# Two transformer stacks on one core: the head norm of the second stack's attention, on VectorE whole or in pieces of 256 columns

## The chip, the core and the metric

One core of a Trainium2 chip runs the whole program. The metric is device time in microseconds (us), as a median of several executions. The engines are TensorE (PE in the profile; its weight loads are PEld), VectorE (DVE), ScalarE (ACT), GpSimd (POOL) and SyncE (SP), which issues most of the loads of weights.

## What is computed

Two stacks of two layers each work on 512 tokens of 1,024 features in fp32. The change touches only the attention of the second stack, which also carries 256 context tokens (in its first layer as queries and keys, in its last layer as keys alone):

```python
def diff_attn(q, k, v, lam):                      # 4 heads, each with two query/key halves of 64, values of 128
    s = jnp.einsum('bhqd,bhkd->bhqk', q, k).astype(jnp.float32) * (HEAD_DIM ** -0.5)
    a = jax.nn.softmax(s, axis=-1).reshape(b, N_HEADS, 2, nq, nk)
    w = a[:, :, 0] - lam * a[:, :, 1]
    return jnp.einsum('bhqk,bhkd->bhqd', w.astype(v.dtype), v)

def head_out(o, g_sub, lam_init):                 # the head norm
    o = rms_norm(o, g_sub) * (1.0 - lam_init)
...
        mix = jnp.concatenate([pool_mixer(u, w_pool[l], s_pool[l]),
                               head_out(o_att, g_subln[l], lam_init)], axis=-1)
        x = x + ga * (mix @ w_out[l])
```

## The kernel before

Activations lie with features on the 128 partitions and tokens along the columns: columns 0 to 255 are the context, 256 to 767 the tokens (`TC` = 256, `TA` = 768). Every large product is three passes of TensorE over a split of each operand into a high and a low part (lines L575 to L577). GpSimd splits each slab of weights in turn (L515 the high part, L518 the low part) as soon as TensorE has finished with the slab whose place it takes. The order on each engine is written by hand: every engine has an `attend2` of its own that walks the same list of units, and semaphores join them.

A unit is one head and one tile of 128 queries. The first layer of the second stack (L = 0) has 6 units for each of the 4 heads: two context tiles with 256 keys, then four token tiles with 768 keys. The last layer (L = 1) has only the four token tiles, so 4 units for each head. For a unit u the work is:

- TensorE computes the scores of both halves into PSUM banks 0 to 2 (L954). It may only do so once ScalarE has read the scores of unit u-1.
- VectorE takes the maximum, `maximum` (L2337), ScalarE the two exponentials (L1643, L1647).
- VectorE joins the two maps, `combine` (L2347 reciprocal of 2 sums, L2349, L2352).
- TensorE turns the map (L969), ScalarE copies it out (L1658: one copy for a 256-key map, two for a 768-key map, and in its order the second stands behind the exponentials of unit u+1), TensorE multiplies it with the values (L983).

Between these steps, in three slots for each unit, lies other work (`extra`, paced by `pace`): TensorE's projections of the next head's queries, keys and values into a ring of three PSUM banks, with their rotation. For the rotation TensorE swaps halves (L665) and VectorE multiplies and adds (`rope2`, L1937, L1939, L1942); the bank is free for the next projection only after L1942. VectorE has the window sums of the pool mixer there too (`centred_mean`, L2299 to L2324), and behind the last heads the low parts of the output's operand (`low`).

When the last unit of head n is multiplied, its head norm starts. ScalarE writes the output to `q_t[:, n]` and its square to `k_t[:, n]` (whose keys are no longer needed), TensorE sums the square over the partitions (L995), ScalarE takes the root into `k_t` (L1676: token columns first, then, for L = 0, the context columns). VectorE waits for the last root, takes the reciprocal of all columns (L2358) and multiplies (L2360). In VectorE's loop the head norm stands at the end of the iteration after the one in which the head ended: behind that unit's combination and its two later slots, ahead of the next maximum. Call the head's last unit e. VectorE's order is then

```python
maximum(e+1); combine(e+1); rest of the slots of e+1; head_norm; maximum(e+2); combine(e+2) ...
```

Nothing needs the result of the head norm until the output projection in the last head's slots, except for the last head, whose norm stands at the very end of the attention. There are 8 head norms: 4 of 768 columns (L = 0), 4 of 512 columns (L = 1).

Of the kernel before, what the change touches and what calls it, by code (L numbers as in the profile page):

```python
# [21 lines left out]
TA = TC + T  # L22
# [141 lines left out]
def steps2(head, last):  # L164

    return sum(STEPS2[kind] + (0 if last or kind not in "qu" else 4) for kind, m in TILES2[head])
# [32 lines left out]
def pace(steps, total, slots):  # L199

    done = 0
    for i in range(slots):
        for _ in range(done, (i + 1) * total // slots):
            next(steps)
        done = (i + 1) * total // slots
        if i == slots - 1:
            for _ in steps:
                pass
        yield
# [113 lines left out]
def program(nc, counts, a):  # L323
    tensor, vector, scalar, gpsimd, sync = nc.tensor, nc.vector, nc.scalar, nc.gpsimd, nc.sync
    scope = ExitStack()

    def signal(name, step=1):
        return Signal(nc, scope, name, counts, step)
# [16 lines left out]
    lams = top.take("lambda_columns", [P, 8])  # L345
# [60 lines left out]
    q_t = att2.take("q2", [P, NH2, TA])  # L406
    k_t = att2.take("k2", [P, NH2, TA])
# [43 lines left out]
    paired, inverted, scaled, h_lo = (signal(n) for n in ("squares_paired", "inverted", "scaled", "h_split"))  # L451
# [753 lines left out]
    def units2(last):  # L1205
        units = []
        for n in range(NH2):
            if not last:
                units += [(n, t, TC, 0) for t in range(2)]
            units += [(n, t, TA, 1) for t in range(2, TA // P)]  # L1210
        return units
# [572 lines left out]
    def vector_engine():  # L1784
# [458 lines left out]
        def second_layer(L):  # L2243
# [9 lines left out]
            rope2(L, 1, 0, 1)  # L2253
            rope2(L, 2, 0, 3)
            attend2(L, last, segs)
            outs = [(TC, TA, 1, TC)] if last else [(TC, TA, 1, TC), (0, TC, 2, 0)]
            vector.wait_ge(*mod_done.at(*(("up2", L - 1) if L else ("feed", DEPTH - 1))))
# [70 lines left out]
        def attend2(L, last, segs):  # L2328
            units = units2(last)
            per = len(units) // NH2  # L2330
            x0 = TC if last else 0
            ring = 0

            def maximum(u):
                n, t, nk, _ = units[u]
                vector.wait_ge(*scored.at(L, "2", u))
                vector.tensor_reduce(  # L2337
                    stat2[:, u % 4, 0:2],
                    psum[:, 0:2 * max(nk, 512)].rearrange("p (m k) -> p m k", m=2)[:, :, 0:nk],
                    AX.X, ALU.max, negate=True).then_inc(*maxed.up(L, "2", u))  # L2340

            def combine(u):
                n, t, nk, _ = units[u]
                rs, rr = stat2[:, u % 4, 2:4], stat2[:, u % 4, 4:6]
                e0, e1 = prob2[:, u % 2, 0:nk], second2[:, 0:nk]
                vector.wait_ge(*probs.at(L, "2", u))
                vector.reciprocal(rr, rs).then_inc(*inverted.up(L, "2", u))  # L2347
                vector.wait_ge(*inverted.at(L, "2", u))
                vector.tensor_scalar(e1, e1, rr[:, 1:2], lams[:, 5:6], ALU.mult,  # L2349
                                     ALU.mult).then_inc(*dve_misc.up(L, "second_map", u))  # L2350
                vector.wait_ge(*dve_misc.at(L, "second_map", u))
                vector.scalar_tensor_tensor(out=e0, in0=e0, scalar=rr[:, 0:1], in1=e1, op0=ALU.mult,  # L2352
                                            op1=ALU.add).then_inc(*normed.up(L, "2", u))

            def head_norm(n):
                ho, rms = q_t[:, n, x0:TA], k_t[:, n, x0:TA]
                vector.wait_ge(*rooted.at(L, "head", n, 0))
                vector.reciprocal(rms, rms).then_inc(*inverted.up(L, "head", n))  # L2358
                vector.wait_ge(*inverted.at(L, "head", n))
                vector.scalar_tensor_tensor(out=ho, in0=ho, scalar=lams[:, 6:7], in1=rms, op0=ALU.mult,  # L2360
                                            op1=ALU.mult).then_inc(*scaled.up(L, "head", n))

            def low(k):
                vector.wait_ge(*o_hi.at(L, "2", k))
# [54 lines left out]
            ended = []  # L2419
            for s in range(len(units) + 1):  # L2420
                if s % per == 0 and s < len(units):
                    n = s // per
                    fill = pace(extra(n), steps2(n, last), 3 * per)
                if s < len(units):
                    maximum(s)
                for part in range(3):
                    next(fill, None)
                    if part == 0 and s < len(units):
                        combine(s)
                while ended:  # L2430
                    head_norm(ended.pop())
                if s and units[s - 1][3] and units[s - 1][1] == TA // P - 1:
                    ended.append(units[s - 1][0])
            while ended:
                head_norm(ended.pop())
            low(7)

        angles()
# [142 lines left out]
```

## Time and profile before

| what | value |
|---|---|
| median of 3 runs | 3588.51 us (3586.37 to 3588.83) |
| the profiled execution | 3586.86 us, its span in the trace 3585.5 us |
| PE busy | 3408.4 us, 95% of the span |
| POOL, DVE, ACT busy | 1578.2, 1323.7 and 800.8 us |
| mean granted clock of TensorE | 0.982 |

The span runs from the first to the last instruction; 1.4 us of the execution lie outside it. A busy time counts the instructions of one engine, which overlap with those of the others. The attention of the second stack runs from about 2040 to 2300 us (L = 0) and from about 2960 to 3170 us (L = 1).

### The profile page before, as it was taken

What the parts mean: (1) busy time and instruction counts of PE and PEld (TensorE: products, weight loads), DVE (VectorE), ACT (ScalarE), POOL (GpSimd) and SP (SyncE); (2) the same over time, 40 slices, a digit from 0 to 9 for tenths busy, and PEclk for the clock granted to TensorE, in tenths of its full rate; (3) what the DMA queues carried; (4) which work ended last, traced back from release to release, by engine and by line L of the source; (5) the groups of instructions that cost most, each with busy time, mean ns of one, the idle gap of its engine ahead of it and who ended that gap; (6) DMA issues with size and microseconds to landing.
All of it is one profiled execution on the core that took longest, in us unless ns stands there. A gap on an engine that the chain in (4) does not pass through costs nothing.

```text
span 3585.5 us, 42527 instructions
## 1 busy us (share of the span) xinstructions
PE 3408.4 (95%) x17440; PEld 2687.4 (75%) x17452; DVE 1323.7 (37%) x2282; ACT 800.8 (22%) x1608; POOL 1578.2 (44%) x996
## 2 busy tenths in 40 slices
PE   6989999999999999999999898889999989889998
PEld 4667777788866677777778787778888878667886
DVE  5843313311159333132122665641211255551113
ACT  2243411100022444111011334320110123420111
POOL 3413356566544134664565421233333333235664
PEclk8999999999999999999999999999999999999999
DMA  6434122333233441335442210132432311114321
GB/s 203 135 127 143 48 90 94 106 94 94 84 99 124 130 130 48 94 103 161 130 141 83 81 48 24 37 106 71 141 118 95 106 51 59 36 47 138 97 94 59
DMA packets 403370, 346.80 MB, mean 97 GB/s; under 512 B 9701, under 2 KB 400613, under 8 KB 403178
## 3 DMA queue, kind: packets, MB, share of 16 engines
q1 hardware_dynamic: 395328, 336.62, 30.0%
q10 hardware_dynamic: 7850, 7.47, 0.7%
q8 instruction: 139, 2.28, 0.3%
q14 instruction: 53, 0.43, 0.0%
HBM read 341.96 MB, written 2.10 MB: 96 GB/s over the span
## 4 chain that ended last, share of the span: by engine, by line
PE 88%; DVE 6%; ACT 3%; issue 1%; DMA 1%; POOL 1%; ACTq 0%; DVEq 0%; POOLq 0%
PE psum L575 26%; PE psum L577 25%; PE psum L576 25%; PE psum L557 2%; PE psum L837 2%; PE psum L983 1%; PE psum L954 1%; PE psum L825 1%; PE psum L769 1%; DVE psum L1838 1%; PE psum L665 1%; DVE k L2358 1%; PE psum L812 1%; PE psum L810 1%; PE psum L814 1%
## 5 line engine op out<-in xcount | busy, mean ns | idle before, releaser
L515 POOL TENSOR_SCALAR weights_hi<-raw_weights 128x1024 fp32r<-128x1024 f32 (+3 forms) x496 | 498.0, 1004 | 1937.1 <-PE psum L577 1617.7
L575 PE MATMUL psum<-h_hi,weights_hi 128*128 128x512 f32 (+1 forms) x2832 | 1139.5, 402 | 70.0 <-DVE h_lo L1880 54.2
L518 POOL TENSOR_TENSOR weights_lo<-raw_weights,weights_hi 128x1024 fp32r<-128x1024 f32 (+3 forms) x496 | 1089.0, 2196 | 41.4
L577 PE MATMUL psum<-h_hi,weights_lo 128*128 128x512 f32 (+1 forms) x2832 | 1077.8, 381 | 0.0
L576 PE MATMUL psum<-h_lo,weights_hi 128*128 128x512 f32 (+1 forms) x2832 | 1076.3, 380 | 0.0
L575 PEld LDWEIGHTS psum<-h_hi,weights_hi 128*128 128x128 f32 x2832 | 538.8, 190 | 230.7 <-issue 111.1
L576 PEld LDWEIGHTS psum<-h_lo,weights_hi 128*128 128x128 f32 x2832 | 538.9, 190 | 117.1 <-issue 15.6
L577 PEld LDWEIGHTS psum<-h_hi,weights_lo 128*128 128x128 f32 x2832 | 537.9, 190 | 109.0
L575 PE MATMUL psum<-hidden_hi,weights_hi 128*128 128x512 f32 (+1 forms) x1120 | 411.7, 368 | 0.0
L576 PE MATMUL psum<-hidden_lo,weights_hi 128*128 128x512 f32 (+1 forms) x1120 | 411.3, 367 | 0.0
L577 PE MATMUL psum<-hidden_hi,weights_lo 128*128 128x512 f32 (+1 forms) x1120 | 410.8, 367 | 0.0
L2135 DVE SCALAR_TENSOR_TENSOR x<-psum,mod,x 128x512 f32<-128x512 f32 (+1 forms) x184 | 123.3, 691 | 559.2 <-PE psum L577 559.1
L575 PEld LDWEIGHTS psum<-hidden_hi,weights_hi 128*128 128x128 f32 x1120 | 211.4, 189 | 37.7 <-issue 0.8
L577 PEld LDWEIGHTS psum<-hidden_hi,weights_lo 128*128 128x128 f32 x1120 | 211.3, 189 | 36.3
L576 PEld LDWEIGHTS psum<-hidden_lo,weights_hi 128*128 128x128 f32 x1120 | 211.4, 189 | 36.1
L1616 ACT ACTIVATE relu_squared<-psum 128x256 f32<-128x256 f32 (+1 forms) x96 | 47.1, 525 | 661.9 <-PE psum L577 661.9
L2271 DVE TENSOR_TENSOR psum<-psum,relu_squared 128x256 f32<-128x256 f32 (+1 forms) x96 | 58.4, 610 | 330.6 <-ACT relu_squared L1616 328.9
L557 PE MATMUL psum<-raw_weights,cond 128*32 128x256 f32 x1536 | 109.7, 408 | 22.5 <-DVE cond L1796 13.8
L2150 DVE TENSOR_TENSOR silu<-psum,silu 128x512 f32<-128x512 f32 x44 | 30.4, 692 | 200.2 <-ACT silu L1497 200.2
L1497 ACT ACTIVATE silu<-psum 128x512 f32<-128x512 f32 x44 | 26.4, 599 | 339.7 <-PE psum L577 339.7
L1250 ACT ACTIVATE squares<-x 128x512 f32<-128x512 f32 (+1 forms) x80 | 43.3, 563 | 244.1 <-DVE x L2135 210.8
L557 PEld LDWEIGHTS psum<-raw_weights,cond 128*32 128x32 f32 x1536 | 42.6, 114 | 72.8 <-issue 41.0
(284 smaller groups left out, 3599.3 us busy)
## 6 DMA issues: line engine op xcount, KB each, us to landing
raw_weights<-in_ada_w SPq DMA_DIRECT2D x96, 1024.0 KB, 5.3
raw_weights<-in_w_mlp SPq DMA_DIRECT2D x64, 1024.0 KB, 5.2
raw_weights<-in_w_in SPq DMA_DIRECT2D x54, 1024.0 KB, 5.4
raw_weights<-in_w_ffn_in SPq DMA_DIRECT2D x88, 512.0 KB, 5.2
raw_weights<-in_w_out SPq DMA_DIRECT2D x16, 1024.0 KB, 5.0
raw_weights<-in_w_ffn_out SPq DMA_DIRECT2D x16, 1024.0 KB, 5.0
raw_weights<-in_w_in SPq DMA_DIRECT2D x30, 512.0 KB, 4.2
raw_weights<-in_w_branch SPq DMA_DIRECT2D x56, 128.0 KB, 2.2
```

The costliest lines, as they stand in the source:

```text
L515: gpsimd.tensor_scalar(whi[:, r, c0:c1], raw[:, raw_slot, c0:c1], 1.0, 1.0, ALU.mult, ALU.mult).then_inc(*split_hi.up(*key, half))
L518: gpsimd.tensor_tensor(wlo[:, r, c0:c1], raw[:, raw_slot, c0:c1], whi[:, r, c0:c1].bitcast(F32), ALU.subtract).then_inc(*split.up(*key, half))
L557: ins = tensor.matmul(bank[bk][32 * g:32 * g + 32, 0:256], cond[:, 4 * kk + g, at:at + 32], view[:, 4 * kk + g, :], start=c == 0 and kk == ...
L575: tensor.matmul(out, sh, mh, start=first, stop=False, skip_group_check=shared)
L576: tensor.matmul(out, sh, ml, start=False, stop=False, skip_group_check=shared)
L577: return tensor.matmul(out, sl, mh, start=False, stop=last, skip_group_check=shared)
L665: tensor.matmul(bank[bk][:, 0:n], matrix, x, start=True, stop=True).then_inc(*swapped.up(*key))
L837: ins = tensor.matmul(bank[3][:, i * P:i * P + P], values_of(kind, h // 2)[:, j, :], probt[:, q, j * P:j * P + P], start=j == 0, stop=j == i)
L1250: scalar.activation(part_of(work, 1 + (k + 1) % 2 if k else 0, x0, x1), X[:, k, x0:x1], ACT.Square, scale=scale).then_inc(*squared.up(whic ...
L1616: scalar.activation(sq2[:, count % 2, 0:c1 - c0], bank[bk][:, 0:c1 - c0], ACT.Relu).then_inc(*moved.up(L, "relu2", chunk, n, s))
L2135: vector.scalar_tensor_tensor(out=xs, in0=bank[bk][:, at:at + x1 - x0], scalar=mod[:, part * 8 + n, m:m + 1], in1=xs, op0=ALU.mult, op1=AL ...
L2271: vector.tensor_tensor(x, x, sq2[:, count % 2, 0:c1 - c0], ALU.mult).then_inc(*dve_misc.up(L, "square", count))
```

## The change

The reciprocals and multiplications of a head norm are cut into pieces of 256 columns: three for L = 0, two for L = 1. `head_norm` becomes a generator, and VectorE's loop takes steps of it, two steps in each of the second and third slots of a unit, behind the slot's other work. The generator does all reciprocals first, then all multiplications. For the last head nothing follows, and all pieces are made in a row at the end.

```diff
             def head_norm(n):
-                ho, rms = q_t[:, n, x0:TA], k_t[:, n, x0:TA]
+                cuts = [(c, c + 256) for c in range(x0, TA, 256)]
                 vector.wait_ge(*rooted.at(L, "head", n, 0))
-                vector.reciprocal(rms, rms).then_inc(*inverted.up(L, "head", n))
-                vector.wait_ge(*inverted.at(L, "head", n))
-                vector.scalar_tensor_tensor(out=ho, in0=ho, scalar=lams[:, 6:7], in1=rms, op0=ALU.mult,
-                                            op1=ALU.mult).then_inc(*scaled.up(L, "head", n))
+                for c0, c1 in cuts:
+                    rms = k_t[:, n, c0:c1]
+                    vector.reciprocal(rms, rms).then_inc(*inverted.up(L, "head", n, c0))
+                    yield
+                for c0, c1 in cuts:
+                    ho, rms = q_t[:, n, c0:c1], k_t[:, n, c0:c1]
+                    vector.wait_ge(*inverted.at(L, "head", n, c0))
+                    vector.scalar_tensor_tensor(out=ho, in0=ho, scalar=lams[:, 6:7], in1=rms, op0=ALU.mult,
+                                                op1=ALU.mult).then_inc(*scaled.up(L, "head", n))
+                    if c1 < TA:
+                        yield
+
+            def head_step():
+                if ended and next(ended[0], "done") == "done":
+                    ended.pop(0)
...
                     next(fill, None)
                     if part == 0 and s < len(units):
                         combine(s)
-                while ended:
-                    head_norm(ended.pop())
+                    else:
+                        head_step()
+                        head_step()
                 if s and units[s - 1][3] and units[s - 1][1] == TA // P - 1:
-                    ended.append(units[s - 1][0])
+                    ended.append(head_norm(units[s - 1][0]))
             while ended:
-                head_norm(ended.pop())
+                head_step()
             low(7)
```

The other engines' orders are the same. VectorE has 24 more instructions in the program. The first place is VectorE at the end of head 0 in L = 0, where `q_108` and `k_109` are `q_t` and `k_t`. Before:

```order
L2352 SCALAR_TENSOR_TENSOR maps<-maps,softmax_stats_106,second_map 128x256
L1937 TENSOR_TENSOR psum<-psum,axial_sin 128x512
L1939 TENSOR_TENSOR q_108<-q_108,axial_cos 128x512
L1942 TENSOR_TENSOR q_108<-psum,q_108 128x512
L2358 RECIPROCAL k_109<-k_109 128x768
L2360 SCALAR_TENSOR_TENSOR q_108<-q_108,lambda_columns,k_109 128x768
L2337 TENSOR_REDUCE softmax_stats_106<-psum 128x2
L2347 RECIPROCAL softmax_stats_106<-softmax_stats_106 128x2
L2349 TENSOR_SCALAR second_map<-second_map,softmax_stats_106,lambda_columns 128x768
L2352 SCALAR_TENSOR_TENSOR maps<-maps,softmax_stats_106,second_map 128x768
L2337 TENSOR_REDUCE softmax_stats_106<-psum 128x2
```

And now, at the same place:

```order
L2360 RECIPROCAL k_109<-k_109 128x256 x2
L1937 TENSOR_TENSOR psum<-psum,axial_sin 128x512
L1939 TENSOR_TENSOR q_108<-q_108,axial_cos 128x512
L1942 TENSOR_TENSOR q_108<-psum,q_108 128x512
L2360 RECIPROCAL k_109<-k_109 128x256
L2365 SCALAR_TENSOR_TENSOR q_108<-q_108,lambda_columns,k_109 128x256
L2337 TENSOR_REDUCE softmax_stats_106<-psum 128x2
L2347 RECIPROCAL softmax_stats_106<-softmax_stats_106 128x2
L2349 TENSOR_SCALAR second_map<-second_map,softmax_stats_106,lambda_columns 128x768
L2352 SCALAR_TENSOR_TENSOR maps<-maps,softmax_stats_106,second_map 128x768
L2365 SCALAR_TENSOR_TENSOR q_108<-q_108,lambda_columns,k_109 128x256 x2
L2337 TENSOR_REDUCE softmax_stats_106<-psum 128x2
```

All three reciprocals and one multiplication still stand ahead of the next maximum, two of the reciprocals now ahead of the rotation; two multiplications stand behind the next combination, ahead of the maximum after that.

The second place is VectorE at the end of head 0 in L = 1. Before:

```order
L2352 SCALAR_TENSOR_TENSOR maps<-maps,softmax_stats_106,second_map 128x768
L1937 TENSOR_TENSOR psum<-psum,axial_sin 128x512
L1939 TENSOR_TENSOR k_109<-k_109,axial_cos 128x512
L1942 TENSOR_TENSOR k_109<-psum,k_109 128x512
L2299 TENSOR_TENSOR windows<-pool_in 128x799
L2307 TENSOR_TENSOR windows<-windows 128x797
L2358 RECIPROCAL k_109<-k_109 128x512
L2360 SCALAR_TENSOR_TENSOR q_108<-q_108,lambda_columns,k_109 128x512
L2337 TENSOR_REDUCE softmax_stats_106<-psum 128x2
```

And now:

```order
L2352 SCALAR_TENSOR_TENSOR maps<-maps,softmax_stats_106,second_map 128x768
L2360 RECIPROCAL k_109<-k_109 128x256 x2
L1937 TENSOR_TENSOR psum<-psum,axial_sin 128x512
L1939 TENSOR_TENSOR k_109<-k_109,axial_cos 128x512
L1942 TENSOR_TENSOR k_109<-psum,k_109 128x512
L2299 TENSOR_TENSOR windows<-pool_in 128x799
L2307 TENSOR_TENSOR windows<-windows 128x797
L2365 SCALAR_TENSOR_TENSOR q_108<-q_108,lambda_columns,k_109 128x256 x2
L2337 TENSOR_REDUCE softmax_stats_106<-psum 128x2
```

Here all four pieces still stand ahead of the next maximum, the reciprocals ahead of the rotation of the keys instead of behind it. It is the same for heads 1 and 2 of L = 1, but that the rotation of head 1 is still ahead of the reciprocals. For heads 1 and 2 of L = 0 three reciprocals and one multiplication stand ahead of the next maximum and two multiplications behind the next combination.

## Rows read from the trace of the kernel before

**Rows 1.** The page: busy time, share of the span and instructions of each engine.

```profile
PE 3408.4 (95%) x17440; PEld 2687.4 (75%) x17452; DVE 1323.7 (37%) x2282; ACT 800.8 (22%) x1608; POOL 1578.2 (44%) x996
```

**Rows 2.** Timeline, TensorE alone: start, duration, instruction, idle time before and its releaser.

```profile
2133.38 1.56 PE L954 MATMUL psum<-k,q 64*128 64x256 f32 x8 [1.88 <-ACT second_map L1647]
2140.46 0.39 PE L575 MATMUL psum<-weights_hi,h_hi 128*128 128x256 f32 x1 [1.19 <-DVE k L1942]
2191.95 1.56 PE L954 MATMUL psum<-k,q 64*128 64x256 f32 x8 [3.64 <-ACT second_map L1647]
2200.14 1.60 PE L983 MATMUL psum<-map_t,v 128*128 128x128 f32 x12 [1.53 <-ACT map_t L1658]
2245.45 2.93 PE L954 MATMUL psum<-k,q 64*128 64x256 f32 x8 [6.36 <-ACT second_map L1647]
3051.66 2.93 PE L983 MATMUL psum<-map_t,v 128*128 128x128 f32 x12 [4.13 <-ACT map_t L1658]
3099.72 1.61 PE L983 MATMUL psum<-map_t,v 128*128 128x128 f32 x12 [2.96 <-ACT map_t L1658]
```

**Rows 3.** VectorE's groups by form, 2000 to 3200 us: busy, mean ns.

```profile
L2358 DVE RECIPROCAL k<-k 128x768 f32<-128x768 f32 x4 | 19.8, 4952 | 11.8 <-ACT k L1676 11.8
L2358 DVE RECIPROCAL k<-k 128x512 f32<-128x512 f32 x4 | 13.4, 3346 | 7.3 <-ACT k L1676 7.3
```

**Rows 4.** Timeline around the end of head 0, L = 0.

```profile
2120.91 0.48 DVE L2352 SCALAR_TENSOR_TENSOR maps<-maps,softmax_stats,second_map 128x256 f32<-128x256 f32 x1
...
2121.82 0.47 ACT L1676 ACTIVATE k<-psum,eps 128x256 f32<-128x256 f32 x1
...
2123.66 4.94 DVE L2358 RECIPROCAL k<-k 128x768 f32<-128x768 f32 x1
2128.64 1.02 DVE L2360 SCALAR_TENSOR_TENSOR q<-q,lambda_columns,k 128x768 f32<-128x768 f32 x1
2129.57 1.75 DVE L2337 TENSOR_REDUCE softmax_stats<-psum 128x2 f32<-128x1536 f32 x1
...
2135.06 1.68 DVE L2352 SCALAR_TENSOR_TENSOR maps<-maps,softmax_stats,second_map 128x768 f32<-128x768 f32 x1
...
2136.02 2.97 POOL L518 TENSOR_TENSOR weights_lo<-raw_weights,weights_hi 128x1024 fp32r<-128x1024 f32 x1
...
2136.66 1.74 DVE L2337 TENSOR_REDUCE softmax_stats<-psum 128x2 f32<-128x1536 f32 x1
...
2139.71 0.69 DVE L1942 TENSOR_TENSOR k<-psum,k 128x512 f32<-128x512 f32 x1
```

**Rows 5.** Timeline, VectorE, around the ends of heads 1 and 2, L = 0.

```profile
2195.68 1.75 DVE L2337 TENSOR_REDUCE softmax_stats<-psum 128x2 f32<-128x1536 f32 x1
...
2239.76 1.97 DVE L2360 SCALAR_TENSOR_TENSOR q<-q,lambda_columns,k 128x768 f32<-128x768 f32 x1
```

**Rows 6.** Timeline around the end of head 0, L = 1.

```profile
3034.51 2.55 POOL L518 TENSOR_TENSOR weights_lo<-raw_weights,weights_hi 128x1024 fp32r<-128x1024 f32 x1
...
3034.88 3.00 DVE L2352 SCALAR_TENSOR_TENSOR maps<-maps,softmax_stats,second_map 128x768 f32<-128x768 f32 x1
...
3037.80 0.69 DVE L1937 TENSOR_TENSOR psum<-psum,axial_sin 128x512 f32<-128x512 f32 x1
...
3038.86 2.71 POOL L518 TENSOR_TENSOR weights_lo<-raw_weights,weights_hi 128x1024 fp32r<-128x1024 f32 x1
...
3040.03 2.38 DVE L2299 TENSOR_TENSOR windows<-pool_in 128x799 f32<-128x799 f32 x1
...
3040.17 0.19 PEld L575 LDWEIGHTS psum<-weights_hi,h_hi 128*128 128x128 f32 x1 [0.19 <-DVE k L1942]
...
3047.41 1.75 DVE L2337 TENSOR_REDUCE softmax_stats<-psum 128x2 f32<-128x1536 f32 x1
```

**Rows 7.** Busy times by stretch: from:to, length, PE, PEld, DVE, ACT, POOL, PEclk, DMA.

```profile
2192.00:2196.00 4.00, 4.00 (x21) 3.14 (x22) 3.82 (x6) 0.49 (x2) 0.00 (x0) 1.00 0.00 0
3051.70:3057.20 5.50, 5.50 (x20) 4.30 (x20) 1.30 (x2) 0.18 (x1) 0.00 (x0) 0.50 0.00 0
```

## The prediction

> **What bounds the kernel now.** I read the page first: TensorE is busy 95% of the span, so a change on VectorE counts only where TensorE waits for it [rows 1]. Then I read TensorE's timeline behind the end of each head and looked at what it waited for. Six head norms stand inside the loop (heads 0 to 2 of both layers). Behind five of them TensorE waits for something that the late maximum holds up [rows 2]:
>
> - L = 0, head 0: 1.88 us for the scores' banks, then 1.19 us for a PSUM bank that the keys' rotation frees.
> - L = 0, head 1: 3.64 us and 1.53 us. L = 0, head 2: 6.36 us.
> - L = 1, head 0: 4.13 us for the second copy of a map, which stands behind the exponentials on ScalarE. L = 1, head 1: 2.96 us. Behind head 2 there is no such wait.
>
> At each place the question is when the next maximum starts, and what else in VectorE's queue now starts later.
>
> **Prices of the pieces.** A reciprocal takes 4.952 us for 768 columns and 3.346 for 512 [rows 3]: 1.606 us for 256 columns and 0.13 us fixed, so a piece takes 1.74 us. An instruction starts about 0.08 us before the one ahead of it ends (2128.64 + 1.02 against 2129.57) [rows 4], so pieces follow each other every 1.66 us. A multiplication of 256 columns has the form of the combination that took 0.48 us [rows 4], so 0.40 us each in a row. The whole norm of L = 0 took 2129.57 - 2123.66 = 5.91 us [rows 4]; in pieces it is 3 x 1.66 + 3 x 0.40 = 6.18, that is 0.27 us more. For L = 1, 3.35 + 0.75 less the overlaps is 4.05 us; 2 x 1.66 + 2 x 0.40 = 4.12, that is 0.07 more. The gap between the dependent reciprocal and multiplication is gone, which pays for part of it. The other side of the trade is an old warning of the Trainium skill, page "VectorE: DVE Perf Modes", sections "The TRN2 errata" and "Rules for kernel authors": minimise the number of VectorE instructions, since each pays a fixed cost (58 cycles in its table, 0.06 us; about 150 by its own measurement, 0.16 us). By that, 24 more instructions would cost an estimated 1.5 to 3.7 us of VectorE; the two forms measured here give 0.13 us each before the overlap, and my sum goes by them.
>
> **L = 0, head 0.** The root of the context columns ends at 2122.29 [rows 4]. Before, the rotation ran first and the norm began at 2123.66. Now two reciprocals run from 2122.33 to 2125.65, the rotation (2.0 us, as the one from 2138.40 to 2140.40) to 2127.65, one reciprocal and one multiplication (2.06 us) to 2129.7. The maximum starts at 2129.7 against 2129.57: nothing won. Behind the next combination, which ends at 2136.74, stand the two other multiplications. Here lies the one large term. Both inputs of a multiplication are in SBUF, and where GpSimd is in an instruction such a one stands still: with L518 running from 3034.51, a combination took 3.00 us, where the same shape takes 1.02 [rows 4, 6]. GpSimd's L518 was issued at 2136.02, while VectorE was in its combination, and ended at 2138.99 [rows 4]. It is in line first, so I take it to run first: the multiplications end at 2139.8, and the maximum that started at 2136.66 starts 3.1 us later. The rotation of the keys behind it ended at 2140.40 and TensorE waited for it [rows 2, 4]: TensorE's wait of 1.19 us becomes 4.3 us. That is longer than the 4.13 that brought the half clock, so I add one stretch, 2.7 us. Term: +3.1 and +2.7. If VectorE goes first, it is 0.8 + 0.1 = +0.9 and no stretch.
>
> **L = 0, heads 1 and 2.** Three reciprocals and one multiplication stand ahead of the maximum: 5.38 against 5.91, so it is 0.53 us earlier and the first wait shrinks by that. Then the two multiplications (0.80 us) stand ahead of the maximum after it, which VectorE starts without idling already (2195.68) [rows 5], and from which the second wait (1.53) hangs: +0.27. The same for head 2, where the longer multiplication (1.97 us) met GpSimd and the shorter will too [rows 5]: +0.27. Sum +0.5.
>
> **L = 1, head 0.** The reciprocals move ahead of the keys' rotation. The rotation started at 3037.80 and ends 3.3 us later now, at 3043.2. TensorE needed its bank and started as soon as it was free, at 3040.17 [rows 6], so it stops there for 3.1 us more. This lies ahead of the wait of 4.13 us and is paid out of it. Meanwhile GpSimd's L518, from 3038.86, had held the first window sum (2.38 us, where 768 columns at the same rate take 1.02) and a little of the rotation (2.3 us to TensorE's start at 3040.17, in place of 2.0) [rows 4, 6]; 3.3 us later both miss it, which gives back 1.4 + 0.3 less the pieces' 0.07, so 1.6 us: the maximum starts at about 3045.8 in place of 3047.41. TensorE, 3.1 us late, would reach its product with the values at 3047.53 + 3.05 = 3050.6, when the map is there: 1.1 us earlier than 3051.66. And the 4.13 us have become one wait of some 3.2 us, under the 3.64 that kept the full clock, so this half-clock stretch goes. Term: -1.1 and -2.7. If the clock falls at 3.2 us after all, TensorE works slowly up to the product and it is +1.6 in place of -3.8.
>
> **L = 1, heads 1 and 2, and the last heads.** All pieces are ahead of the maximum: +0.07 each, +0.1. The last heads' pieces cost 0.27 and 0.07 us; TensorE has the products of six other operand rows in between, so 0, at most +0.4. Signals and waits of the pieces are VectorE's own. No DMA, no slab and no other engine's order is moved.
>
> **Sum.** 3.1 + 2.7 + 0.5 - 1.1 - 2.7 + 0.1 = +2.6 us. The profiled execution took 3586.86 us, so 3589.5; it lay 1.65 us under the median of the three runs, and the median becomes 3588.5 + 2.6 = 3591.1 us. The three runs differ by 2.5 us, and 0.2% (7.2 us) is about what a measurement of this kernel can tell from no change.
>
> **Rivals.**
>
> 1. *The pieces free the maximum.* VectorE idles between each maximum and its combination, while ScalarE makes the exponentials; if the norm lay in such gaps the 21.7 us of waits and two stretches of 2.7 us would go: 3588.5 - 27 = 3561 us. Against it: the order shows 5.38 of 6.18 us still ahead of the next maximum in L = 0, and all of it in L = 1. Something like half would need the order to be other than it is. Chance 0.04.
> 2. *The rotation's bank starves TensorE.* The place is L = 1, head 0: TensorE stops at 3040 for 3.2 us, and if the clock falls there, the sum is 3.1 + 2.7 + 0.5 + 1.6 + 0.1 = +8.0, 3596.5 us, slower than before. It decides from an idle time between 3.64 us (full clock) and 4.13 us (half), so a rotation 0.5 us later than I think is enough. For it: two reciprocals now stand ahead of every rotation that shares their slots. Against it: the 3.64 of [rows 2]. Chance 0.13.
> 3. *VectorE goes before GpSimd at head 0 of L = 0.* Then +0.9 and no stretch there: 0.9 + 0.5 - 3.8 + 0.1 = -2.3, 3586.2 us. For it: its multiplications are queued directly behind the combination. Against it: in 2136.02 to 2138.99 GpSimd's instruction was waiting already. The Trainium skill, page "SBUF — State Buffer", section "SBUF: two separate sides", says that whichever starts first has the shared ports for its whole instruction and the other is blocked; by that the case is decided by who is issued first, which is GpSimd. Chance 0.15.
> 4. *Nothing of the large terms*: the holds and stretches shift against each other and only the pieces' fixed costs stay, +0.6, 3589.1 us. Chance 0.2.
>
> The forecast has 0.48. **How the numbers follow.** The forecast, rivals 3 and 4 lie within 0.2%. Rival 1 is faster, with some 0.01 for scatter; rival 2 is just above the bound, and part of it falls below. So faster 0.05, same 0.83, slower 0.12. The range goes from rival 3 less the scatter of the runs (3584) to rival 2 and a little (3598).
>
> **What would show it.** Right: reciprocals of 1.74 us; the maximum at the end of head 0 (L = 0) no earlier against the scores than before; a multiplication of some 2.7 us there, a wait of some 4 us for the rotation, and the half clock behind it; in L = 1, head 0, a wait of 3 us in front of the value tile and the full clock at the products with the values. Wrong: if the six first waits shrink by more than 1 us each; if the multiplications at 2136 take 0.48 us; if the rotations' banks hold TensorE at a place where it had no wait; if moved GpSimd instructions meet other VectorE ones, which I worked out only at these places.

## The result, and the profile after

The changed kernel takes 3592.72 us, the median of 20 executions (3591.53 to 3594.55); the kernel before took 3587.27 us beside it (20 executions, 3585.01 to 3589.47). The ratio is 1.0016, with a 95% interval of 1.0009 to 1.0022: 5.45 us more. That is less than the 7.2 us (0.2%) that the prediction took as the bound of "same". The interval lies above 1, so with this many executions the loss is real. The profiled execution took 3593.38 us with a span of 3592.1, against 3586.86 and 3585.5.

One thing in the listing of the order ahead of the prediction must be put right. A head's last unit e is multiplied with the values while VectorE is at unit e+1, so the norm stood behind the combination of e+2 and ahead of `maximum(e+3)`, one unit later than that listing says. The rows of the order and the prediction's steps show it rightly.

The page, first line of its busy times:

```profile
PE 3415.7 (95%) x17440; PEld 2694.0 (75%) x17452; DVE 1322.0 (37%) x2306; ACT 800.1 (22%) x1608; POOL 1578.2 (44%) x996
```

TensorE has the same 17,440 instructions as in [rows 1] and is busy 7.3 us longer: it is slower in places, it does not do more. VectorE has its 24 additional instructions and is busy no longer.

TensorE's timeline of the changed kernel at the places of [rows 2] (start, duration, instruction, idle time before and its releaser):

```profile
2133.74 1.56 PE L954 MATMUL psum<-k,q 64*128 64x256 f32 x8 [1.84 <-ACT second_map L1647]
2143.80 0.58 PE L575 MATMUL psum<-weights_hi,h_hi 128*128 128x256 f32 x1 [4.15 <-DVE k L1942]
2196.83 2.93 PE L954 MATMUL psum<-k,q 64*128 64x256 f32 x8 [2.88 <-ACT second_map L1647]
2205.82 1.60 PE L983 MATMUL psum<-map_t,v 128*128 128x128 f32 x12 [0.74 <-ACT map_t L1658]
2250.56 2.93 PE L954 MATMUL psum<-k,q 64*128 64x256 f32 x8 [5.83 <-ACT second_map L1647]
2261.39 1.85 PE L1022 MATMUL psum<-pool_in,ada_rows 128*128 128x512 f32 x2 [2.23 <-ACT map_t L1658]
3051.82 0.39 PE L575 MATMUL psum<-weights_hi,h_hi 128*128 128x256 f32 x1 [3.01 <-DVE k L1942]
3104.47 1.60 PE L983 MATMUL psum<-map_t,v 128*128 128x128 f32 x12 [1.59 <-ACT map_t L1658]
```

Line by line against [rows 2]: the scores' wait at head 0 is as it was (1.88, now 1.84), the keys' rotation is waited for 4.15 in place of 1.19 us, the scores of heads 1 and 2 wait 0.76 and 0.53 us less, head 1's second wait is 0.79 us shorter (1.53, now 0.74), a wait of 2.23 us stands where head 2 had one of 0.56 (below), and in L = 1 a wait of 3.01 us for a rotation's bank has come in front of the value tile while the one of 4.13 us is gone. The products behind the waits of 2.88 and 5.83 us show the duration of the half clock (2.93 us for eight scores, against 1.56).

VectorE's groups by form, 2000 to 3200 us, for [rows 3] (busy, mean ns):

```profile
L2360 DVE RECIPROCAL k<-k 128x256 f32<-128x256 f32 x20 | 33.5, 1719 | 20.0 <-ACT k L1676 20.0
L2365 DVE SCALAR_TENSOR_TENSOR q<-q,lambda_columns,k 128x256 f32<-128x256 f32 x20 | 11.6, 614 | 0.0
```

The piece of a reciprocal takes 1.72 us, as worked out (1.74). The 20 pieces are busy 33.5 us, where the 8 whole reciprocals took 33.2. The multiplications have a mean of 614 ns where 480 were expected: some are held.

VectorE and GpSimd at the end of head 0, L = 0, for [rows 4]:

```profile
2122.73 3.37 DVE L2360 RECIPROCAL k<-k 128x256 f32<-128x256 f32 x2 [0.93 <-ACT k L1676]
...
2127.98 1.74 DVE L2360 RECIPROCAL k<-k 128x256 f32<-128x256 f32 x1
...
2129.94 1.75 DVE L2337 TENSOR_REDUCE softmax_stats<-psum 128x2 f32<-128x1536 f32 x1
...
2136.44 2.97 POOL L518 TENSOR_TENSOR weights_lo<-raw_weights,weights_hi 128x1024 fp32r<-128x1024 f32 x1
...
2137.08 3.01 DVE L2365 SCALAR_TENSOR_TENSOR q<-q,lambda_columns,k 128x256 f32<-128x256 f32 x2
...
2140.01 1.74 DVE L2337 TENSOR_REDUCE softmax_stats<-psum 128x2 f32<-128x1536 f32 x1
...
2143.05 0.69 DVE L1942 TENSOR_TENSOR k<-psum,k 128x512 f32<-128x512 f32 x1
```

The maximum starts at 2129.94, 0.37 us later than before, which is how much later the whole attention began: nothing won. Two multiplications of 256 columns take 3.01 us together; the second starts at 2139.61, just after L518 has ended (2139.41), so the first was held by 2.1 us. The maximum behind them starts at 2140.01 against 2136.66.

End of head 0 in L = 1, for [rows 6]:

```profile
3043.15 2.55 POOL L518 TENSOR_TENSOR weights_lo<-raw_weights,weights_hi 128x1024 fp32r<-128x1024 f32 x1
3043.52 3.00 DVE L2352 SCALAR_TENSOR_TENSOR maps<-maps,softmax_stats,second_map 128x768 f32<-128x768 f32 x1
...
3046.44 3.35 DVE L2360 RECIPROCAL k<-k 128x256 f32<-128x256 f32 x2
...
3049.71 0.67 DVE L1937 TENSOR_TENSOR psum<-psum,axial_sin 128x512 f32<-128x512 f32 x1
...
3051.68 0.98 DVE L2299 TENSOR_TENSOR windows<-pool_in 128x799 f32<-128x799 f32 x1
...
3054.39 1.75 DVE L2337 TENSOR_REDUCE softmax_stats<-psum 128x2 f32<-128x1536 f32 x1
```

The window sum takes 0.98 us, where L518 had held it for 2.38. The maximum starts 6.98 us later than in [rows 6], and the maximum ahead of it 8.61 us later (3033.01 against 3024.40): 1.6 us given back, as in the prediction.

The row of before that answers to the one at 2261.39, TensorE's timeline of the kernel before:

```profile
2255.49 1.10 PE L1022 MATMUL psum<-pool_in,ada_rows 128*128 128x512 f32 x2 [0.56 <-ACT map_t L1658]
```

The granted clock in two stretches, for [rows 7] (the seventh value behind the time is PEclk):

```profile
2143.80:2149.00 5.20, 5.20 (x24) 5.20 (x25) 5.06 (x11) 0.50 (x2) 0.00 (x0) 0.50 0.00 0
3051.80:3058.00 6.20, 6.18 (x52) 6.19 (x53) 6.09 (x9) 2.41 (x6) 0.00 (x0) 1.00 0.39 137
```

Behind the wait of 4.15 us the clock is at half, behind the one of 3.01 us it is full.

### The profile page after: what moved, and what is told of

Same layout as the page of the kernel before. It is cut to its first block, busy times and chain, and to the rows that moved or that the text cites. A ratio compares the mean times of both kernels' runs of the same rounds, so it can differ in the third digit from the quotient of the medians.

```text
span 3592.1 us, 42551 instructions
## 1 busy us (share of the span) xinstructions
PE 3415.7 (95%) x17440; PEld 2694.0 (75%) x17452; DVE 1322.0 (37%) x2306; ACT 800.1 (22%) x1608; POOL 1578.2 (44%) x996
## 4 chain that ended last, share of the span: by engine, by line
PE 88%; DVE 5%; ACT 3%; issue 1%; DMA 1%; POOL 1%; ACTq 0%; DVEq 0%; SPq 0%; POOLq 0%
PE psum L575 26%; PE psum L577 25%; PE psum L576 25%; PE psum L557 2%; PE psum L837 2%; PE psum L983 1%; PE psum L954 1%; PE psum L825 1%; PE psum L769 1%; DVE psum L1838 1%; PE psum L665 1%; PE psum L812 1%; PE psum L810 1%; DVE k L2360 1%; PE psum L814 1%
## 5 line engine op out<-in xcount | busy, mean ns | idle before, releaser
L518 POOL TENSOR_TENSOR weights_lo<-raw_weights,weights_hi 128x1024 fp32r<-128x1024 f32 (+3 forms) x496 | 1088.5, 2195 | 41.4
L2154 DVE TENSOR_TENSOR psum<-psum,silu 128x512 f32<-128x512 f32 x44 | 30.8, 700 | 179.8 <-PE psum L577 179.6
```

The costliest lines, as they stand in the source:

```text
L518: gpsimd.tensor_tensor(wlo[:, r, c0:c1], raw[:, raw_slot, c0:c1], whi[:, r, c0:c1].bitcast(F32), ALU.subtract).then_inc(*split.up(*key, half))
```

## The experiments

Each kernel is the changed one with the edit shown. Times are medians; the kernel before ran beside them, 3587.86 us for the first four and 3587.28 for `cut_in_place`, `mult_whole`, `gaps` and `gap_whole`. `gaps` has 5 executions, `gap_whole` 6, the other six 11. To say where time went I use one measure throughout: the start of the same unit's maximum (L2337, 40 of them) in two traces. The difference of these shifts over a head is what the head cost. A trace is one execution, though, and need not lie at the median: those of `whole_early` and `cut_in_place` lie 4.0 us above theirs (1.4 and 2.4 us of shift are there ahead of the first maximum), that of `l1_pieces` 2.9 us below (1.5 of it ahead of the first maximum). So a head's cost says what happened there once, and the medians say what a kernel costs.

**L = 0 alone, L = 1 alone** (`l0_pieces`; `l1_pieces` has 1 and 0 exchanged):

```diff
-                cuts = [(c, c + 256) for c in range(x0, TA, 256)]
+                cuts = [(c, c + 256) for c in range(x0, TA, 256)] if L == 0 else [(x0, TA)]
...
-                    else:
+                    elif L == 0:
                         head_step()
                         head_step()
+                while ended and L != 0:
+                    head_step()
```

> Pieces in L = 0 only, the norms of L = 1 whole and at their old place. Theory (the change is a sum of local terms: +5.2 us at head 0 of L = 0 from multiplications that stand still behind GpSimd and the half clock after it, about 0 at head 1, +1.9 at head 2, -4.1 at head 0 of L = 1): this kernel is 7.1 us slower than before, and the wait of 4.1 us at head 0 of L = 1 with its half clock is back. Rival (half of the change's 5.5 us lies outside the attention, in where the instructions or loads fall): 9 to 10 us slower, or the markers behind 3200 us shift by more than those of the attention.

> Pieces in L = 1 only, the norms of L = 0 as before. Theory of local terms: 3.9 us faster than before (-4.1 at head 0 from the wait in front of the value tile in place of the longer one behind it, +0.2 at head 1, 0 at head 2), with the full clock at the products with the values. Rival of an outside cost: only 1 to 2 us faster or no change.

Measured: 3594.34 us (1.0018, 1.0009 to 1.0027), +6.5; and 3587.03 us (0.9998, 0.9989 to 1.0007), -0.8. Together +5.7, and the whole change has +5.45, so the medians add up, within intervals of some 3 us to either side. The loss is all in L = 0. With whole norms in L = 1 the old wait is back (3059.30, 4.14 us, with a 2.93 us product). In `l1_pieces` head 0 gave back 2.5 us by the maxima, not 3.8, because the wait that should have kept the full clock did not:

```profile
3041.63 0.39 PE L575 MATMUL psum<-weights_hi,h_hi 128*128 128x256 f32 x1 [2.98 <-DVE k L1942]
```

```profile
3041.63:3045.63 4.00, 4.00 (x21) 4.00 (x22) 3.96 (x5) 0.44 (x1) 0.00 (x0) 0.57 0.63 221
```

The same wait for the same bank as at 3051.82 above (2.98 and 3.01 us), once with half the clock behind it and once with all of it. For `l1_pieces` 3.9 us less was expected and the rival had 1 to 2 us or nothing; by its number the rival came out. The trace has 1.6 us of the difference at this place, by the clock, and 1.2 us behind the attention in code that is the same, which is what the rival named.

**The whole norm, only earlier** (`whole_early`):

```diff
-                cuts = [(c, c + 256) for c in range(x0, TA, 256)]
+                cuts = [(x0, TA)]
```

> One cut of all columns with the change's stepping: the norm is whole but stands in the second slot, ahead of the rotation that the third slot brings. Theory (cutting costs 0.3 us a norm, the place is what counts): the gain of about 4 us at head 0 of L = 1 is there too if the 3.8 us wait for the rotation's bank keeps the full clock, and in L = 0, with no multiplication behind the combination, head 0 loses 1 to 2 us; in total 2 to 4 us faster than the change. Rival (a wait of 3.8 us brings the half clock): the gain at head 0 of L = 1 is 1 us or less.

Measured: 3589.72 us (1.0005, 0.9996 to 1.0014), 3.0 us under the changed kernel, as expected, but not by the steps expected. L = 0, head 0, costs 5.2 us here too (1 to 2 were expected), though no multiplication stands behind a combination. The norm sits ahead of the queries' rotation, and TensorE waits 2.21 us for it. The combination then meets L518 and takes 2.99 us, and an instruction of the keys' rotation meets the next L518 and takes 1.72 in place of 0.68. TensorE waits 2.92 us for that rotation, and the clock behind is half (0.50 for 5 us):

```profile
2136.19 2.54 POOL L518 TENSOR_TENSOR weights_lo<-raw_weights,weights_hi 128x1024 fp32r<-128x1024 f32 x1
2136.55 2.99 DVE L2352 SCALAR_TENSOR_TENSOR maps<-maps,softmax_stats,second_map 128x768 f32<-128x768 f32 x1
...
2140.55 2.37 POOL L518 TENSOR_TENSOR weights_lo<-raw_weights,weights_hi 128x1024 fp32r<-128x1024 f32 x1
...
2141.74 1.72 DVE L1939 TENSOR_TENSOR k<-k,axial_cos 128x512 f32<-128x512 f32 x1
...
2144.31 0.58 PE L575 MATMUL psum<-weights_hi,h_hi 128*128 128x256 f32 x1 [2.92 <-DVE k L1942]
```

So what the norm costs there is a question of which instruction stands where L518 starts, not of the cut. In L = 1 neither the theory nor its rival held: the wait for the rotation's bank at head 0 is 3.75 us, the clock behind it is half (0.55 over 3.7 us), and head 0 still gave back 1.8 us, not 4 and not under 1.

**All pieces ahead of the next maximum** (`all_ahead`):

```diff
-                        head_step()
-                        head_step()
+                        for _ in range(3):
+                            head_step()
```

> As the change, but three steps in each slot, so that in L = 0 too every piece stands ahead of the next maximum and nothing behind the next combination. Theory (the large loss at head 0 of L = 0 is the hold by GpSimd and the half clock): its wait for the keys' rotation returns to 1 to 2 us at full clock, the loss there is about 1 to 2 us instead of 5.2, and the kernel is 3 us faster than the change or more. Rival (the rotation behind three reciprocals costs as much, since TensorE waits for its bank, or head 1's first wait grows to 3.9 us and brings the half clock): within 1 us of the change.

Measured: 3591.78 us (1.0010, 1.0001 to 1.0019), 0.9 us under the changed kernel, a difference that the two intervals do not tell from nothing; the theory wanted 3 us. Its step at head 0 of L = 0 held: that head costs 1.4 us in place of 5.3, with a wait of 1.77 us at the full clock, so the two multiplications behind the combination are the large term there. But head 2 costs 3.1 us, since all three now meet GpSimd:

```profile
2240.20 2.34 POOL L518 TENSOR_TENSOR weights_lo<-raw_weights,weights_hi 128x1024 fp32r<-128x1024 f32 x1
2241.29 5.18 DVE L2365 SCALAR_TENSOR_TENSOR q<-q,lambda_columns,k 128x256 f32<-128x256 f32 x3
...
2243.80 2.39 POOL L518 TENSOR_TENSOR weights_lo<-raw_weights,weights_hi 128x1024 fp32r<-128x1024 f32 x1
...
2250.19 2.93 PE L954 MATMUL psum<-k,q 64*128 64x256 f32 x8 [9.48 <-ACT second_map L1647]
```

The one multiplication of 768 columns took 1.97 us here [rows 5]; three of 256 take 5.18 (1.53, 1.25 and 2.56 us), because the last of them reaches into the second L518 as well, and the wait of 6.36 us becomes 9.48.

**The cut alone, at the old place** (`cut_in_place`), and **reciprocals in pieces, the multiplication whole** (`mult_whole`, with three steps for each slot as above):

```diff
-                    else:
-                        head_step()
-                        head_step()
+                while ended:
+                    head_step()
```

```diff
...
-                for c0, c1 in cuts:
-                    ho, rms = q_t[:, n, c0:c1], k_t[:, n, c0:c1]
-                    vector.wait_ge(*inverted.at(L, "head", n, c0))
+                ho, rms = q_t[:, n, x0:TA], k_t[:, n, x0:TA]
+                vector.wait_ge(*inverted.at(L, "head", n, TA - 256))
...
```

> The pieces of the change, all in a row at the old place of the norm, in both layers. This is the price of the cutting alone. Theory: 0.27 us a norm in L = 0 and 0.07 us in L = 1 where TensorE waits, plus what GpSimd holds the two further multiplications at head 2 of L = 0 (up to 3 us, as 5.2 us for three of them in the kernel with all pieces ahead): 1 to 4 us slower than before, with no new wait for a rotation. Rival (the order of pieces and rotation is of no matter, the pieces themselves cost the 5 us): 5 us slower or more.

> As the kernel with all pieces ahead of the next maximum, but the multiplication of a norm whole. Theory (each cut multiplication is a chance to stand still behind GpSimd): at head 2 of L = 0 the multiplication takes 1 to 2 us in place of 5.2 us for three, TensorE's wait of 9.5 us there falls to 6 to 7 us, and the kernel is about 3 us faster than that one. Rival: the wait there stays above 9 us.

Measured: 3590.09 us (1.0007, 0.9999 to 1.0016) and 3589.92 us (1.0009, 1.0000 to 1.0017). The cut alone costs 2.8 us, inside the 1 to 4 expected. With it head 2 of L = 0 costs 3.1 us by the maxima (the same 5.18 us of held multiplications, the same wait of 9.48 us), head 2 of L = 1 costs 0.8, and the other four between +0.3 and -0.3: more instructions cost next to nothing but where they are held. With the multiplication whole, head 2 costs 0.0 us and TensorE waits 6.36 us again. That settles the 5.18 us: it is the number of multiplications in front of GpSimd, not their place. The whole one starts 1.21 us behind the start of L518, the first of the three 1.09 and 1.10 us behind it.

```profile
2243.75 1.95 DVE L2364 SCALAR_TENSOR_TENSOR q<-q,lambda_columns,k 128x768 f32<-128x768 f32 x1
```

But `mult_whole` is only 1.9 us faster than `all_ahead`, where 3 were expected, and in its trace other heads lose by the clock. Head 0 of L = 0 costs 2.9 us (a wait of 2.08 us for the keys' rotation, and 0.57 of the clock over 4 us behind it). Head 1 costs 1.1 us: its scores waited 3.64 us, to the hundredth as in the kernel before, and had half the clock where that had all of it [rows 7].

```profile
2194.79 2.93 PE L954 MATMUL psum<-k,q 64*128 64x256 f32 x8 [3.64 <-ACT second_map L1647]
```

```profile
2194.79:2200.20 5.41, 5.41 (x14) 3.75 (x15) 5.23 (x7) 0.12 (x1) 0.00 (x0) 0.50 0.00 0
```

**The two kernels once more** (`change_again`, `before_again`), unaltered, for the clock:

> The changed kernel once more, unaltered, for the clock alone. Its first profile showed at the end of L = 0, head 0, a wait of 4.15 us for the keys' rotation with half the clock behind it, one of 2.88 us at head 1 with half the clock, and one of 3.01 us at L = 1, head 0, with the full clock. Theory A: the wait's length decides, so the clocks are the same as in the first profile at every place. Theory B: for a wait of 2 to 4 us the clock that follows also depends on the execution, so at least one of the waits of about 3 us comes with the other clock than the first time, by 1.3 to 2.7 us of time at the place. The order, the waits' lengths and the starts of the maxima up to the first such place repeat within 0.1 us in both.

> The kernel before once more, unaltered, for the clock alone. Its first profile showed waits of 3.64 us (L = 0, head 1) with the full clock, 6.36 (head 2) and 4.13 us (L = 1, head 0) with half the clock, and 2.96 us (L = 1, head 1) with the full clock. Theory A, the wait's length decides: the same clocks. Theory B, it depends on the execution too for waits of 2 to 4 us: the 3.64 or the 2.96 may come with half the clock, and the span differs from 3585.5 by about as much as the places with another clock make, 1.3 to 2.7 us each.

Measured: 3592.54 and 3588.07 us, one execution each. TensorE's timeline and clock in the second execution of the changed kernel:

```profile
3049.47 0.56 PE L575 MATMUL psum<-weights_hi,h_hi 128*128 128x256 f32 x1 [2.99 <-DVE k L1942]
...
3103.38 2.26 PE L983 MATMUL psum<-map_t,v 128*128 128x128 f32 x12 [2.85 <-ACT map_t L1658]
```

```profile
3049.50:3055.50 6.00, 6.00 (x38) 6.00 (x39) 5.90 (x9) 2.25 (x4) 0.00 (x0) 0.72 0.41 144
```

The waits of L = 0 have the same lengths within 0.01 us and the same clocks as the first time (half behind 4.15, 2.87 and 5.82 us), but for the last, which is 2.04 us in place of 2.23 and again has half the clock behind it. In L = 1 the 2.99 us have half the clock behind them, where 3.01 us had the full one. That took 1.5 us at head 0 (-2.5 by the maxima, -4.0 in the first execution). At head 1 the wait is 2.85 us in place of 1.59, the products take 2.26 us in place of 1.60, and another 1.6 us go. In the kernel before, the second execution has the same clocks as the first; its wait of 3.64 us (3.61 now) kept the full clock both times. So for waits of about 3 us the length does not decide the clock: theory B holds for the changed kernel. The kernel before alone shows nothing against either, but the 3.64 us of `mult_whole` had half the clock, so up to there at least the length does not decide. The Trainium skill, page "TensorE: Matmul & The Clock Gate", section "Part 1: The HAM clock gate", says of a kernel's first products that the moment of the transition depends on where they fall in the gate's own timing, which does not start anew with the kernel. No run here shows that timing; one wait with either clock behind it does not contradict it.

**The pieces between a maximum and its combination** (`gaps`), where VectorE waits for the exponentials, by a small table: key is (last layer, head 2, place, iterations since the head ended), value the number of steps. "gap" is ahead of `combine(s)` in the first slot, "end" behind the last slot.

```diff
+            plan = {(False, False, "gap", 2): 1, (False, False, "gap", 3): 1, (False, False, "gap", 4): 1,
+                    (False, False, "gap", 5): 3,
+                    (False, True, "end", 1): 1, (False, True, "gap", 2): 1, (False, True, "gap", 3): 4,
+                    (True, False, "gap", 1): 1, (True, False, "gap", 2): 1, (True, False, "gap", 3): 2,
+                    (True, True, "gap", 1): 1, (True, True, "gap", 2): 3}
...
                     if part == 0 and s < len(units):
+                        head_step(s, "gap")
                         combine(s)
-                    else:
-                        head_step()
-                        head_step()
+                head_step(s, "end")
```

and **the whole norm in one such gap** (`gap_whole`), with `cuts = [(x0, TA)]` and

```diff
+            plan = {(False, False, "gap", 2): 2, (False, True, "gap", 2): 2,
+                    (True, False, "gap", 1): 2, (True, True, "gap", 1): 2}
```

> The same pieces, placed by a table: one reciprocal in each gap between a maximum and its combination (VectorE idles 1.9 us and more there for the exponentials), the multiplications in one gap after them; for head 2 of L = 0 one reciprocal at the old place. Theory (TensorE's waits behind the heads come from what stands between a combination and the next maximum, and a piece in the other gap is free): the 21.7 us of waits shrink to 5 us or less and the half-clock stretches at heads 2 of L = 0 and 0 of L = 1 go, so 15 to 25 us faster than before, 3562 to 3573 us. Rival (the combination is as much on the path as the maximum, or the pieces meet GpSimd): less than 8 us faster.

> As the kernel with the gaps, but each norm whole in one gap between maximum and combination. Theory (a reciprocal of 5 us does not fit a gap of 1.9 us and makes the combination 4 us late, which TensorE's next turning of a map waits for): 5 to 15 us slower than the kernel with pieces in the gaps, between that and before. Rival (cutting is of no use, only the gap is): within 2 us of the kernel with pieces in the gaps.

Measured: **3571.62 us (0.9956, 0.9942 to 0.9969)**, 15.7 us under the kernel before, and 3576.76 us (0.9971, 0.9959 to 0.9982), 10.5 us under it. Both beat both kernels. The time of `gaps` is in the range expected (15 to 25 us less), that of `gap_whole` too (5 to 15 us above `gaps`). TensorE's waits of over 1 us that are left in `gaps` in the stretches of [rows 2]:

```profile
2141.30 0.38 PE L575 MATMUL psum<-weights_hi,h_hi 128*128 128x256 f32 x1 [3.07 <-DVE k L1942]
...
2198.55 1.60 PE L983 MATMUL psum<-map_t,v 128*128 128x128 f32 x12 [1.22 <-ACT map_t L1658]
...
2238.58 1.56 PE L954 MATMUL psum<-k,q 64*128 64x256 f32 x8 [1.11 <-ACT second_map L1647]
2241.49 0.66 PE L969 MATMUL psum<-constants,maps 128*128 128x128 f32 x4 [1.35 <-DVE maps L2352]
2244.60 0.47 PE L575 MATMUL psum<-h_hi,weights_hi 128*128 128x512 f32 x1 [2.46 <-DVE h_lo L2395]
```

9.2 us in place of 21.7 (5 or less were expected), and in L = 1 none but those that the kernel before has too and that the 21.7 leaves out (1.92 and 1.91 us, and 5.35 where it has 4.39). By the maxima the heads of L = 0 give +1.5, -4.0 and -2.1 us, those of L = 1 -6.7, -3.2 and -0.8. Head 0 of L = 0 does not gain: its maximum starts at 2125.93 in place of 2129.57 and the scores no longer wait, but GpSimd's slab then starts as the combination does (L518 at 2133.19, L2352 at 2133.55 for 3.00 us in place of 1.68), and the keys' rotation is late again, with 3.07 us of waiting and part of the stretch behind it at half the clock (0.65 over 4.8 us). In `gap_whole` a norm of 768 columns is longer than the gap. At head 2 it pushes the combination into GpSimd, and TensorE waits 5.25 us for the map:

```profile
2241.59 1.25 DVE L2365 SCALAR_TENSOR_TENSOR q<-q,lambda_columns,k 128x768 f32<-128x768 f32 x1
2242.12 2.92 POOL L518 TENSOR_TENSOR weights_lo<-raw_weights,weights_hi 128x1024 fp32r<-128x1024 f32 x1
...
2242.95 2.51 DVE L2349 TENSOR_SCALAR second_map<-second_map,softmax_stats,lambda_columns 128x768 f32<-128x768 f32 x1
...
2246.57 1.11 PE L969 MATMUL psum<-constants,maps 128*128 128x128 f32 x4 [5.25 <-DVE maps L2352]
```

By the maxima the two kernels are alike in L = 1 (-6.7, -3.2 and -0.9 us in `gap_whole`). In L = 0 `gap_whole` has +2.2, -1.9 and -0.9. So the gap is worth two thirds of the gain, and the pieces, once they lie in gaps, another 5.1 us; in the two traces 4 of them lie in L = 0, where the norm is longest.

## Why the prediction was right, and where its terms were not

The forecast was +2.6 us and 3591.1; the medians differ by 5.45 us and the median is 3592.72. It came out as "same" and inside the range, by the mechanism foreseen: nearly all of the norm still ahead of the next maximum, multiplications held at head 0 of L = 0, a hold and a half-clock stretch saved at head 0 of L = 1. The sum was half of what the medians show. Two terms were mis-sized. Ahead of, between and behind the attentions, where the sum had nothing, 3.3 us lie in the first execution and -0.4 in the second. By the maxima, in us:

| place | forecast | first execution | second |
|---|---|---|---|
| ahead of the first maximum | 0 | +0.4 | -0.9 |
| L = 0, head 0 | +5.8 | +5.3 | +5.6 |
| L = 0, head 1 | +0.27 | 0.0 | 0.0 |
| L = 0, head 2 | +0.27 | +1.9 | +1.8 |
| between the two attentions | 0 | +1.0 | -0.2 |
| L = 1, head 0 | -3.8 | -4.0 | -2.5 |
| L = 1, heads 1 and 2 | +0.1 | +0.1 | +1.2 |
| from the first maximum to the last | +2.6 | +4.3 | +5.9 |
| behind the last maximum | 0 | +1.9 | +0.7 |
| the whole span | +2.6 | +6.6 | +5.7 |

- **The pieces' prices** were right (1.72 against 1.74 us), and so, within 0.25 us, were the starts of the maxima: 0.0 at head 0 (+0.1 foreseen), 0.7 and 0.5 us earlier at heads 1 and 2 (0.53 foreseen; waits 0.76 and 0.53 us shorter). The warning against more instructions did not bite: `cut_in_place` loses over 0.3 us at two of six places only, at the larger one through GpSimd, and in the changed kernel the reciprocals are busy 0.3 us longer with 12 more of them (33.5 against 33.2).
- **L = 0, head 0.** The mechanism came as foreseen: held multiplications (3.1 us later maximum foreseen; 2140.01 - 2136.66 less the 0.4 of the start is 3.0), 4.15 us of waiting (4.3 foreseen), half the clock behind. Rival 3, that VectorE goes first, is excluded.
- **L = 0, head 1.** The late multiplications cost nothing: the shorter second wait (0.74 in place of 1.53) takes in the half clock that now follows the 2.88 us. That half clock was not foreseen.
- **L = 0, head 2**: mis-sized, +1.9 in place of +0.27. I stopped at the maximum. It is 0.25 us later, as worked out, but the map that hangs from it was already just in time. Before, TensorE ran on half the clock for some 6.2 us behind the scores' wait; now for some 4.2 us behind the shorter one, so it gets to the map first, waits 2.23 us and falls to half once more (two products of 512 columns in 1.85 in place of 1.10 us). What is late next was to be asked once more.
- **L = 1, head 0**: the step that failed is "under the 3.64 that kept the full clock, so this half-clock stretch goes". The wait was 3.0 us as foreseen, but one row of 3.64 us with the full clock is no threshold: the same wait of 3.0 us had the full clock in one execution of this kernel and half of it in another, and half in `l1_pieces`. Rival 2 named this and drew its line between 3.64 and 4.13 us, which was wrong in place but right in kind. The term is -4.0 or -2.5 by execution, and head 1 goes with it (+0.2 or +1.6). That the first execution met the forecast here is luck as far as the traces tell: of the six traces with the reciprocals or the norm ahead of this rotation (waits of 2.98 to 3.79 us) it alone kept the full clock, and in the others the head gave back 0.6 to 2.5 us.
- **Rival 1**, the pieces in the gap, would have been 27 us. The order excluded it for this change, and the kernel that does it gains 15.7.

The +1.0 between the attentions, where the kernels are the same, is absent in the second execution. Of the time behind the last maximum 0.3 and 0.1 us are there by 3200 us, for the last head's pieces the forecast allowed 0 to 0.4; the rest comes by 3250 us, in code that is the same. There the clock was at half for 10.2 us in the first execution (3210.5 to 3220.7) and for 6.8 us in the second and in the kernel before. Against the kernel before in its own two executions (spans of 3585.5 and 3586.8 us) the two spans lie 5.5 us higher on average, as the medians do. How often each clock occurs at 3050 us was not counted.

## What to carry to other kernels

Cutting an instruction helps only if the pieces lie where their engine idles: look up the idle stretch (here between maximum and combination) and put them there, since a place "behind the next step" may still be ahead of the one that counts. For each moved instruction with two inputs in SBUF, look up what GpSimd does at that time, and then what GpSimd does after the move, for its start moves with TensorE. Follow a delay to the next wait behind it, and where a wait of 2 to 4 us stands in a sum, carry both clocks as a range.

## What the runs showed of the hardware

- Short multiplications in a row behind a GpSimd instruction cost more than a long one. One of 768 columns took 1.97 us against L518, three of 256 took 5.18 us in two kernels, over two L518 of 2.34 and 2.39 us; one by one they took 1.53, 1.25 and 2.56 us. The Trainium skill, page "SBUF — State Buffer", section "SBUF: two separate sides", says that whoever starts first has the shared ports for its whole instruction. The 3.01 us at 2137.08 fit that. For the 5.18 us it would need the second L518 to win between two pieces; the rows fit, but when each was issued was not measured.
- The clock behind a wait of TensorE: half behind all of 4.13 us and more in [rows 2] and here. Between 2 and 4 us the same wait had either. The scores of head 1, L = 0, kept the full clock behind 3.64, 3.61 and 3.61 us (the kernel before twice, `l1_pieces`) and had half of it behind 3.64 (`mult_whole`), 3.61 (`whole_early`) and 3.68 us (`all_ahead`). At head 0 of L = 1 only the 3.01 us of the changed kernel kept it, and 2.98, 2.99, 3.35, 3.75 and 3.79 us did not. One such stretch costs 1.5 to 2.7 us, and it can follow a wait of only 2.23 us, as in the line at 2261.39, or of 1.91 us, as in the kernel before at 3125.21 (0.53 over 3.65 us).
